# Branch norms moved from behind the sample step into the chunks, and merge gates scaled after the product

## What is computed

```python
o = _rmsnorm(o, p['gdn_norm']) * silu(gdn_z)        # per head of 128; the same for GLA
y = y * silu(ssd_z)
y = _rmsnorm(y in 2 groups of 256, p['ssd_norm'])
gates = sigmoid(gate_logits + p['b_merge'])          # gate_logits = h @ w_gate, h = rmsnorm(x) * w
merged = gates[0] * (o_gdn @ w_gdn) + gates[1] * (o_gla @ w_gla) + gates[2] * (o_ssd @ w_ssd)
out = merged @ p['w_out']
```

## Time and profile before

| what | us |
|---|---|
| median of 3 runs | 3509.14 (3504.68 to 3510.58) |
| profiled execution, its own time | 3509.9 |
| span of the trace | 3508.1 |
| chunks of layer 1, from one to the next | 58.6, 58.5, 57.0, 58.5 |
| sample step of layer 1 | 60.2 |
| from the last state added to the first merge matmul | 37.3 |

### The profile page before, as it was taken

One profiled execution on the slowest core, in us unless ns is written; L12 is line 12 of the kernel. 1 busy time (PEld: TensorE's weight loads), 2 busy tenths in 40 slices (PEclk: granted clock), 3 DMA queues, 4 the chain that ended last, 5 costly groups with the idle time before them and its releaser, 6 DMA issues. The chain is left out here.

```text
span 3508.1 us, 68193 instructions
## 1 busy us (share of the span) xinstructions
PE 3243.1 (92%) x26934; PEld 3115.8 (89%) x26934; DVE 1299.5 (37%) x2055; ACT 770.7 (22%) x1363; POOL 1577.9 (45%) x948
## 2 busy tenths in 40 slices
PE   7999989978769998999999999999787699999997
PEld 7999989966659998999999998999666599999997
DVE  3331075456553214331043301753665622143301
ACT  2111032232351112111021101332333411121110
POOL 4565455600015654565545654664000156546553
PEclk9999999999869999999999999999998799999999
DMA  3222222200122221222222222221001222212221
GB/s 124 89 85 85 73 75 89 73 1 1 69 88 82 90 88 63 90 84 85 79 77 90 84 83 62 92 85 60 1 1 69 97 86 89 89 66 84 90 83 64
DMA packets 77981, 259.64 MB, mean 74 GB/s; under 512 B 8576, under 2 KB 10624, under 8 KB 77056
## 3 DMA queue, kind: packets, MB, share of 16 engines
q1 hardware_dynamic: 77536, 256.90, 22.5%
q10 hardware_dynamic: 288, 0.49, 0.1%
HBM read 242.78 MB, written 14.58 MB: 73 GB/s over the span
## 5 line engine op out<-in xcount | busy, mean ns | idle before, releaser
L458 POOL TENSOR_SCALAR wh<-raw 128x1024 fp32r<-128x1024 f32 (+1 forms) x464 | 474.6, 1023 | 1833.0 <-PE ps L499 1178.8
L460 POOL TENSOR_TENSOR wl<-raw,wh 128x1024 fp32r<-128x1024 f32 (+1 forms) x464 | 1069.5, 2305 | 67.8 <-POOL wh L458 0.3
L495 PE MATMUL ps<-hh,wh 128*128 128x272 f32 x4768 | 999.8, 291 | 77.2 <-DVE hl L1679 44.9
L497 PE MATMUL ps<-hl,wh 128*128 128x272 f32 x4768 | 994.7, 290 | 0.0
L499 PE MATMUL ps<-hh,wl 128*128 128x272 f32 x4768 | 989.6, 289 | 0.0
L495 PEld LDWEIGHTS ps<-hh,wh 128*128 128x128 f32 x4768 | 755.4, 190 | 85.7 <-issue 77.0
L497 PEld LDWEIGHTS ps<-hl,wh 128*128 128x128 f32 x4768 | 754.2, 190 | 0.0
L499 PEld LDWEIGHTS ps<-hh,wl 128*128 128x128 f32 x4768 | 753.6, 189 | 0.0
L495 PE MATMUL ps<-ah,wh 128*128 128x272 f32 x1408 | 294.6, 291 | 0.0
L497 PE MATMUL ps<-al,wh 128*128 128x272 f32 x1408 | 290.2, 287 | 0.0
L499 PE MATMUL ps<-ah,wl 128*128 128x272 f32 x1408 | 289.5, 287 | 0.0
(11 more groups left out here) (401 smaller groups left out, 3674.5 us busy)
## 6 DMA issues: line engine op xcount, KB each, us to landing
raw<-in_up SPq DMA_DIRECT2D x176, 512.0 KB, 3.7
raw<-in_win SPq DMA_DIRECT2D x80, 512.0 KB, 3.6
raw<-in_merge SPq DMA_DIRECT2D x96, 384.0 KB, 3.0
raw<-in_down SPq DMA_DIRECT2D x64, 512.0 KB, 3.5
raw<-in_down SPq DMA_DIRECT2D x32, 384.0 KB, 3.1
raw<-in_wout SPq DMA_DIRECT2D x16, 512.0 KB, 3.7
states<-in_in_gdn SPq DMA_DIRECT2D x2, 2048.0 KB, 8.1
proj<-in_in_ssd SPq DMA_DIRECT2D x2, 2048.0 KB, 15.9
```

The source lines that it names most:

```text
L458: pool.tensor_scalar(hi, src, 1.0, 1.0, MULT, MULT).then_inc(hi_done, 1)
L460: pool.tensor_tensor(lo, src, hi.bitcast(F32), SUB).then_inc(lo_done, 1)
L495: pe.matmul(out, high, mh_[:, c], start=a, stop=False)
L497: pe.matmul(out, high, ml_[:, c], start=False, stop=False)
```

## The change

The norms are cut by chunks, and become a fifth generator `n` (`norms_of`) of 12 stages in the same order string. In a chunk the first four stages (n1 to n4) are the norm of branch 1 (GLA) of the chunk before, n5 to n8 that of branch 0 (DeltaNet) of the chunk before, and n9 to n12 that of branch 2 (SSD) of the chunk itself. A norm has, on ACT, Square, Ln, Exp, Copy in its four stages; on PE a matmul in its second; on DVE scale and gate in its third and the low part in its fourth (and for branch 2 the gate product in its first). The first chunk has nothing in n1 to n8. In the sample step n1 to n8 are the last chunk's, and n9 to n12 the norm of the 32 sample columns of all three branches in one.

The places of the norm tiles (`norm_places`) are those of the SSD tiles, so s1 waits until the chunk before is normed. Without the letters n the order strings differ as well: in a chunk l4 and l5 come after g2 instead of before g1, and each later l stage is one slot later; in the sample step s1 comes after n8, g4 and l7 instead of after g1.

The merge takes x times the norm weights as its input, not scaled by the reciprocal root. It can be split in the sample step (`merge_split`, stages h1 to h8) with one ACT and one DVE instruction for each tile. The reciprocal root, `rstd`, is applied to the gate sums instead: for each unit DVE multiplies the sum in PSUM by `rstd` into `sg` and ACT takes the sigmoid of `sg` in place. The loop over `i` is written out on PE, ACT and DVE, and PE waits for all states of the sample step before the merge.

```diff
 
-ORDER = "clclcllggllgslggslgsglgslgslgslglglglgggg"
-
-SAMPLE_ORDER = "clclcl" + "gsl" * 10 + "glgg"
-NORM_ORDER = (2, 0, 1)
+ORDER = "cnlcnlcnlnngngnllngslggslgsglgslgslgslglnglnglnglnggg"
+
+SAMPLE_ORDER = "cnlcnlcnln" + "ngl" * 4 + "sgsl" * 3 + "gg" + "lgsh" * 4 + "nh" * 4
+BRANCHES = 3
+MERGES = 3 * KD
+NORMS = CHUNKS * BRANCHES + 1
 FIRST = 0
 FIRST_BLOCKS = 3
 
 
-def together(order, common, gdn, gla, ssd):
-
-    branch = dict(c=common, g=gdn, l=gla, s=ssd)
+def norm_number(step, b):
+
+    return step.layer * NORMS + (BRANCHES * step.c + (3, 2, 1)[b] if step.prompt else NORMS)
+
+
+def norms_of(norm, step, before, sample_norm=None):
+
+    if before is not None:
+        yield from norm(before, 1)
+        yield from norm(before, 0)
+    else:
+        for turn in range(8):
+            yield
+    if step.prompt:
+        yield from norm(step, 2)
+    else:
+        yield from sample_norm(step)
...
+        norm_places = [[at(f"n_{s}{i}", RING + p, [P, 512]) for s, p in zip(("sq", "rs", "nt"), places)]
+                       for i, places in enumerate(((4096, 6144, 8192), (10240, 0, 2048)))]
...
+                if step.c:
+                    pe.wait_ge(n_["ln"], step.layer * NORMS + BRANCHES * step.c)
...
-            def branch_stats(layer, branch):
-                pe.wait_ge(n_["sq"], value(pe, layer * 3 + (NORM_ORDER.index(branch) + 1)))
-                if branch != NORM_ORDER[0]:
-
-                    pe.wait_ge(n_["ln"], value(pe, layer * 3 + NORM_ORDER.index(branch)))
-                if branch < 2:
...
+            def norm(step, b):
+                q = norm_number(step, b)
+                nsq = norm_places[b % 2][0]
+                bank = 6 + b % 2
+                yield
+                pe.wait_ge(n_["sq"], q)
+                pe.wait_ge(s_["s"], step.once + 2)
+                pe.wait_ge(s_["yc"], step.once + 2)
+                if q > 1:
+                    pe.wait_ge(n_["ln"], q - 1)
...
                 last.then_inc(n_["ss"], 1)
+                yield
+                yield
+                yield
...
-                    step = prompt_step(layer, c)
-                    together(ORDER, common(step), gdn(step), gla(step), ssd(step))
-                step = sample_step(layer)
-                together(SAMPLE_ORDER, common(step), gdn_sample(step), gla_sample(step), ssd_sample(step))
-                for branch in NORM_ORDER:
-                    branch_stats(layer, branch)
-
-
-                pe.wait_ge(n_["ln"], value(pe, layer * 3 + 3))
+                    before, step = step, prompt_step(layer, c)
+                    together(ORDER, common(step), gdn(step), gla(step), ssd(step), norms_of(norm, step, before))
+                before, step = step, sample_step(layer)
+                together(SAMPLE_ORDER, common(step), gdn_sample(step), gla_sample(step), ssd_sample(step),
+                         norms_of(norm, step, before, sample_norm), split_turns())
+
+                for e in (g_, l_, s_):
+                    pe.wait_ge(e["s"], layer * STEPS + STEPS + 1)
 
...
-                        if i is FIRST and u < 2:
-
-                            pe.wait_ge(n_["lo"], value(pe, layer * 3 + (u + 2)))
+                        if i is FIRST and u == 0:
+                            pe.wait_ge(n_["lo"], (layer + 1) * NORMS)
...
+            def norm(step, b):
+                n, q = step.n, norm_number(step, b)
+                nsq, nrs, nt = norm_places[b % 2]
+                if b < 2:
+                    act.wait_ge((g_, l_)[b]["oc"], step.once + 2)
+                    src = proj[:, V[b]:V[b] + 4, step.cols]
+                else:
+                    act.wait_ge(n_["yz"], step.layer * STEPS + step.c + 1)
+                    src = view(nt, 4, n)
+                act.activation(view(nsq, 4, n), src, ACT.Square).then_inc(n_["sq"], 1)
+                yield
+                act.wait_ge(n_["ss"], q)
+                w = 512 if b < 2 else 256
+                act.activation(nrs[:, 0:w], ps[:, 6 + b % 2, 0:w], ACT.Ln, scale=1.0 / (128 if b < 2 else 256), bias=epsc).then_inc(n_["ln"], 1)
+                yield
+                act.wait_ge(n_["ln"], q)
+                act.activation(nrs[:, 0:w], nrs[:, 0:w], ACT.Exp, scale=-0.5).then_inc(n_["rs"], 1)
+                yield
+                act.wait_ge(n_["tz"], q)
+                act.activation(oh[b][:, :, step.cols], view(nt, 4, n), ACT.Copy).then_inc(n_["hi"], 1)
+                yield
...
+            def merge_split(step):
+
+                act.wait_ge(g_["oc"], step.once + 2)
+                act.wait_ge(l_["oc"], step.once + 2)
+                act.wait_ge(g_["sm"], (step.layer + 1) * DEC_BATCH)
+                for k in range(KD):
+                    act.activation(hh[:, k, :], x[:, k, :], ACT.Copy, scale=merge_weights(k)).then_inc(hh_ready, 1)
+                    yield
...
-                        act.wait_ge(blk_done, further(act, layer * BLOCKS + i * 12 + (B_MERGE + 2 * u + 2 + SPLIT)))
-                        act.wait_ge(mac_done, further(act, layer * 24 + i * 6 + (u + 1)))
-                        act.activation(halves(sg[:, u % 2, :]), pair(2 * u % 4), ACT.Sigmoid,
+                        act.wait_ge(gate_done, merge_gates(layer) + i * 6 + u + 1)
+                        act.activation(sg[:, u % 2, :], sg[:, u % 2, :], ACT.Sigmoid,
                                        bias=bm[:, u % 3 * 2 + u // 3:u % 3 * 2 + u // 3 + 1]).then_inc(sg_done, 1)
...
+            def gated(step):
+
+                dst = norm_places[0][2][:, :] if step.prompt else nt_s[:, 8 * step.n:12 * step.n]
+                dve.tensor_tensor(view(dst, 4), proj[:, SX:SX + 4, step.cols], proj[:, SZ:SZ + 4, step.cols], MULT).then_inc(n_["yz"], 1)
...
+            def head_scaled(step, b, nt, nrs):
+                return dve.scalar_tensor_tensor(out=view(nt, 4), in0=proj[:, V[b]:V[b] + 4, step.cols],
+                                                scalar=prm[:, (GDNN, GLAN)[b]:(GDNN, GLAN)[b] + 1],
+                                                in1=view(nrs, 4), op0=MULT, op1=MULT)
+
+            def low_part(step, b, nt):
+                return dve.tensor_tensor(ol[b][:, :, step.cols], view(nt, 4), oh[b][:, :, step.cols].bitcast(F32), SUB)
...
+            def norm(step, b):
+                q = norm_number(step, b)
+                nsq, nrs, nt = norm_places[b % 2]
                 if b == 2:
+                    dve.wait_ge(s_["yc"], step.once + 2)
+                    dve.wait_ge(s_["s"], step.once + 2)
+                    gated(step)
+                yield
+                yield
+                dve.wait_ge(n_["rs"], q)
+                if b == 2:
+                    dve.wait_ge(n_["yz"], step.layer * STEPS + step.c + 1)
+                    state_space_scaled(step, nt, nrs).then_inc(n_["tz"], 1)
                 else:
+                    head_scaled(step, b, nt, nrs).then_inc(n_["t"], 1)
+                    dve.wait_ge(n_["t"], step.layer * (2 * CHUNKS + 1) + 2 * step.c + 2 - b)
+                    dve.tensor_tensor(view(nt, 4), view(nt, 4), proj[:, Z[b]:Z[b] + 4, step.cols], MULT).then_inc(n_["tz"], 1)
+                yield
+                dve.wait_ge(n_["hi"], q)
+                dve.wait_ge(n_["tz"], q)
+                low_part(step, b, nt).then_inc(n_["lo"], 1)
+                yield
+
...
+            def merge_split(step):
+                layer = step.layer
+                dve.wait_ge(g_["ma"], layer * 4 + 4)
+                dve.wait_ge(st_prompt, layer * 48 + 48)
+                for k in range(KD):
+                    dve.wait_ge(hh_ready, layer * (4 * KD) + 2 * KD + k + 1)
+                    dve.scalar_tensor_tensor(out=hl[:, k, :], in0=x[:, k, :], scalar=prm[:, MPRE + k:MPRE + k + 1],
+                                             in1=hh[:, k, :].bitcast(F32), op0=MULT, op1=SUB).then_inc(hl_ready, 1)
...
+                        dve.wait_ge(mac_done, layer * 24 + i * 6 + (u + 1))
+                        dve.tensor_tensor(halves(sg[:, u % 2, :]), pair(2 * u % 4), halves(rstd[:, :]), MULT).then_inc(gate_done, 1)
```

More of the change, by code:

```diff
@@ L1177, in merge @@
                                  True, True).then_inc(blk_done, 1)
-                merge(FIRST)
-                with pe.Fori(1, KD // 2) as i:
+                for i in range(KD // 2):
                     merge(i)
@@ L1616, in _ @@
                 act.preload_act_table_set(LN_EXP)
+                step = None
                 for c in range(CHUNKS):
[L1618 to L1623 removed]
+                    before, step = step, prompt_step(layer, c)
+                    together(ORDER, common(step), gdn(step), gla(step), ssd(step), norms_of(norm, step, before))
+                before, step = step, sample_step(layer)
+                together(SAMPLE_ORDER, common(step), gdn_sample(step), gla_sample(step), ssd_sample(step),
+                         norms_of(norm, step, before, sample_norm), merge_split(step))
+                act.wait_ge(st_out, layer * 48 + 48)
+                for i in range(KD // 2):
```

(35 more changed lines are left out.)

176 lines of the change are left out of this document (78 added, 98 removed).

## The result

The changed kernel takes **3578.07 us** (median of four runs, 3574.45 to 3579.34) where the kernel before takes 3509.23 beside it: a ratio of 1.0197, 95% interval 1.0179 to 1.0214. It is slower by 2%, 69 us. The forecast was 3572 with a range of 3528 to 3602. The profiled execution has a span of 3572.6 us, 64.5 more than before, and a mean clock of TensorE of 0.945 where it was 0.961.

What follows compares the result with a forecast made beforehand. No engine full; chunks bound by handovers between engines. Four chunks +45.7, sample step +10, last state to merge −25.6, merge +0.8: +30.9 us a layer, +62 in two, on 3509.9 gives 3572 us; range 3528 to 3602.

Steps and rivals of the forecast that it cites:

- What bounds a chunk: In each chunk: no engine is full; short steps hand over between engines, so delaying g3 delays the chunk's end.
- Head with norms: Start of three chunks a layer: waits and added work start g3 8.8 us later, +11.3 with the clock loss.
- Clock in that head: PE in the head with norms: half clock after a 5.2 us gap costs 2.5 us, at most 3.7.
- Tail: End of every chunk: n9 to n11 add 2.55 us, or 1.0 if only n11 shows.
- First chunk: First chunk of a layer, no norms ahead: l4 and l5 behind g2 cost 1.6; with the tail +4.2 us.
- Sample step: Sample step: norms ahead and later s stages put the last state +10 us later, between +6.4 and +16.
- From the last state to the merge: Between last state and merge: steady merge starts at +19.6 us instead of +45.2, −25.6, bounds −23 and −28.
- Merge: In the merge: one more DVE instruction per unit shows only at the end, +0.8 us; written-out loop costs nothing.
- Hidden norms: Rival, in the chunks: norms fill DVE's idle time, −18.4 us a layer, 3473 us; chance 0.10.
- Heads that cost only their instructions: Rival, at chunk heads: only 6.7 us of DVE work per chunk with norms, +4 a layer, 3518 us; chance 0.13.
- Half clock on every head: Rival: PE's half clock hits every head and lasts in the sample step, +40 us a layer, 3590; chance 0.15.
- No shorter end: Rival, after the last state: the merge still starts with the norms at +45 us, 3623 us; chance 0.03.

Runs made afterwards that it cites:

- e5: Changed kernel with another chunk order: head up to g3 as before, norms of the chunk before among g4 to g8, s stages later and closer together; 3619.5 us.
- e7: Changed kernel with all norms moved behind the last state, chunk orders nearly as before, root on gate sums and split of `h` kept; 3521.5 us.
- e6: Changed kernel with the four transposes ahead of l_vt made seven times in chunks with norms, to keep PE busy; 3572.4 us.
- e9: Kernel of e6 in which also the eight spreads of s1 are made five times in every chunk, to keep PE busy; 3572.2 us.
- e3: Changed kernel with l4 ahead of g1 again and the later l stages at their old places; 3536.7 us.
- e2: Changed kernel with one swap in the chunk order, l3 ahead of n3; 3575.9 us.
- e1: Kernel before the change with only its merge loops on PE, ACT and DVE written out; ratio 1.0002 to the kernel before.
- e8: Kernel of e7 with each square one norm earlier, the scaled copy one place later and the state-space gate product in the chunk; 3495.95 us.

## Why the prediction was right, and where its sizes were off

**What bounds a chunk.** Right: no engine is full and the waits in order are passed on. e5 and e7 show both ends of it.

**Head with norms, +11.3.** The two waits are where I put them, 5.05 and 3.49 us; I had about 7 and 3.4. In layer 1 g3 comes 9.4 to 10.7 us later, 9.9 on average. I had taken the sums of squares (L622) at the half clock of the last chunk in the earlier trace rows (3.43); here they ran at 1.88, and n3 starts 9.2 us after `cc`, not 11.1. In e6 and e9, where they ran at half clock, the wait is the 6.74 I had in mind.

**Clock in that head, 2.5.** The spread took 1.67 more than at full clock and the norm's sum 0.64: 2.3, in the last chunk of layer 1, and the spread took 3.62 in all six heads. By the rule that I cited, of the Trainium skill ("TensorE: Matmul & The Clock Gate", HAM oscillation), idle gaps of this size throttle every time. The trace agrees for the gap ahead of the spread (5.38 us). Behind the shorter gap of 2.76 both happened: 0.66 over 5 us in e9's last chunk, and the spread at full clock (1.95) in e6's first head.

**Tail, 2.55.** Too small. A chunk takes 3.8 us more from g3 on. The norm there costs 1.4, by e3, less than I had. What the sum put at nothing is that every later l stage comes one slot later, with the half clock as the solve begins: 2.4. So a chunk with norms was to cost 13.85 and cost 13.2, 14.7 and 13.2, 13.7 on average, because a head 1.4 too dear met a tail 1.3 too cheap. That it fits so well is luck.

**First chunk, +4.2.** It was +6.9 in layer 1 and +3.9 in layer 2, 5.4 on average. The difference between layers is the start of the chunk, which the change does not touch:

```profile
713.21 0.16 DVE L1877 COPY cc<-cm 128x128 f32<-128x128 f32 x1
...
722.15 0.42 DVE L2107 TENSOR_TENSOR l_qe<-l_qs,l_eb 128x256 f32<-128x256 f32 x1 [4.19 <-ACT l_er L1421]
...
737.52 0.68 DVE L1940 TENSOR_TENSOR g<-ps,g 128x512 f32<-128x512 f32 x1
```

```profile
719.44 0.42 DVE L2037 TENSOR_TENSOR l_qe<-l_qs,l_eb 128x256 f32<-128x256 f32 x1 [3.37 <-ACT l_er L1370]
...
733.19 0.68 DVE L1870 TENSOR_TENSOR g<-ps,g 128x512 f32<-128x512 f32 x1
```

From `l_qe` to g3 it is 15.37 us after the change and 13.75 before (second view, `cc` at 712.00): the 1.6 that I had for l4 and l5 behind g2. The rest of what was missing is the tail again, 3.8 instead of 2.55, and in layer 1 the 1.5 by which `l_qe` came later. e2, whose first chunk has the changed kernel's order, took 63.4 for it.

**Sample step, +10.** It was +12.1, within 6.4 to 16. e7 splits it: 1.8 for the split of `h`, for which I had 2.0, and some 10 for the norms and the later s stages together.

**From the last state to the merge, −25.6.** It was −25.2, with POOL's first block 14.3 us behind the last state and PE's first matmul 17.3 (1083.45), for which I had 17.2. The loss at half clock behind the long idle, which I put at 2.4, was 2.7 (20.0 less 17.3, with the clock at 0.50 in the window ahead).

**Merge.** The end, +0.8, did not show (−0.1): the last sum of the gates took 2.00 us where 2.48 before. The loop at nothing was right, by e1.

**The rivals.** Hidden norms: in the changed kernel no chunk with norms cost under 13 us. Heads that cost only their instructions: refuted by e3 against the changed kernel, the same instructions in another order and 41 us less. Half clock on every head: seen at every spread, but it did not last into the key products, which started 0.22 us apart, and 3590 was not reached. No shorter end: refuted, by 25.2 us.

## What to carry to other kernels

Where all engines follow one written order, price an inserted stage by what stands behind it in each queue, not by idle shares: 6 us of DVE work cost 7.9 us a chunk. Ask also what had been running beside the stages that it pushes apart. Here the new order of the l stages, which added no instruction, cost another 5.7, of which 2.4 came far behind the place that was changed.

A change that does two things should be priced as two. Taking the norms and the split out of the end gave 25 us a layer, and taking them into the chunks and the sample step cost 60. The root on the gate sums and the early split alone did not give the 25: with them kept and the norms behind the last state again, the end was 6 us longer than before in e7 and 7 us shorter in e8.

Split a measured stage at a point that the change does not touch, as `l_qe` in the first chunk. Single chunks of one code differed by 1.5 us by how their start had run, as much as some of the terms.

## What the runs showed of the hardware

- PE's steady pace, at clock 1.00 in all windows, differed between executions of the same merge loop: 8.96 us a unit in layer 1 of the changed kernel, 9.08 in layer 1 of e3, 9.04 in layer 2 of both.
- A DVE operation with two operands in SBUF took 2.33 us beside POOL's subtraction and 0.68 without it (e8). The Trainium skill ("GPSIMD Engine Reference", Specifications) has the two share their SBUF interfaces, with contention when DVE has two SBUF inputs; the trace agrees.
- PE's extra work in e9 raised its mean clock over the four chunks from 0.83 to 0.92 and took 3.9 us from their 280.6; the kernel's time moved from 3578.1 to 3572.2 us, with overlapping intervals.
